# Expert products in three single passes of high and low parts, one expert after another

## What is computed

```python
order = jnp.argsort(flat_e)
tok = order // TOP_K
sizes = jnp.bincount(flat_e, length=N_EXPERTS).astype(jnp.int32)
xs = h[tok]
a = lax.ragged_dot(xs, w_gate, sizes)
u = lax.ragged_dot(xs, w_up, sizes)
y = lax.ragged_dot(jax.nn.silu(a) * u, w_down, sizes)
y = y * w.reshape(-1)[order][:, None].astype(y.dtype)
return jax.ops.segment_sum(y, tok, num_segments=n)
```

## Time and profile before

| | |
|---|---|
| median of 3 runs | 6089.7 us (6088.2 to 6094.5) |
| the profiled execution | 6090.85 us |
| its span, first to last instruction | 6089.3 us |
| jobs | 74 (36 in layer 0, 38 in layer 1), from 1,184 records of L2059 at 16 a job |
| TensorE busy | 5199.9 us, 85% of the span |
| DMA | 1111.26 MB, mean 182 GB/s |

### The profile page before, as it was taken

One profiled execution on the slowest core, in us unless ns is written; L12 is line 12 of the kernel. 1 busy time (PEld: TensorE's weight loads), 2 busy tenths in 40 slices (PEclk: granted clock), 3 DMA queues, 4 the chain that ended last, 5 costly groups with the idle time before them and its releaser, 6 DMA issues. The chain is left out here.

```text
span 6089.3 us, 76302 instructions
## 1 busy us (share of the span) xinstructions
PE 5199.9 (85%) x27165; PEld 3869.3 (64%) x27165; DVE 2233.9 (37%) x4438; ACT 1677.5 (28%) x2876; POOL 821.7 (13%) x1023
## 2 busy tenths in 40 slices
PE   9588899779789885999991888979879886999995
PEld 1388889669668763444441888978778665444442
DVE  0455155566443432111115552547553333111113
ACT  0244254446322320000001342536542221000000
POOL 0244200440000001000001440006200001000001
PEclk9799999899899997999995999989889998999998
DMA  8432451324332464899976432233343343999997
GB/s 320 175 92 88 145 172 47 95 72 111 135 147 98 167 202 165 326 335 334 334 281 229 144 95 78 68 81 78 90 134 114 143 148 110 343 334 335 334 334 265
DMA packets 610733, 1111.26 MB, mean 182 GB/s; under 512 B 108400, under 2 KB 291984, under 8 KB 610032
## 3 DMA queue, kind: packets, MB, share of 16 engines
q1 hardware_dynamic: 565104, 956.50, 47.0%
q0 software_dynamic: 29504, 94.50, 4.0%
q10 hardware_dynamic: 15936, 57.78, 2.3%
HBM read 908.23 MB, written 200.45 MB: 182 GB/s over the span
## 5 line engine op out<-in xcount | busy, mean ns | idle before, releaser
L642 PE MATMUL project_proj_acc<-project_w_split,project_hT 128*128 128x256 f32 x5472 | 720.0, 291 | 41.0 <-DVE project_w_split L527 41.0
L642 PEld LDWEIGHTS project_proj_acc<-project_w_split,project_hT 128*128 128x128 f32 x5472 | 689.5, 198 | 42.1 <-DVE project_w_split L527 41.8
L1452 PE MATMUL merge_acc<-merge_hT,merge_w_split 128*128 128x512 f32 (+1 forms) x2880 | 633.4, 376 | 20.0 <-issue 16.8
L1452 PEld LDWEIGHTS merge_acc<-merge_hT,merge_w_split 128*128 128x128 f32 x2880 | 507.9, 190 | 128.9 <-issue 22.0
L2059 PE MATMUL experts_gate_acc<-experts_w_gate,experts_rowsT 128*128 128x512 f32 x1184 | 526.0, 597 | 6.9 <-DMA experts_w_up<-in_w_exp_up_dram 6.9
L2046 PE MATMUL experts_result_acc<-experts_w_down,experts_hiddenT 128*128 128x512 f32 x1184 | 520.5, 592 | 2.4 <-DVE experts_hiddenT L2018 2.4
L2064 PE MATMUL experts_up_acc<-experts_w_up,experts_rowsT 128*128 128x512 f32 x1184 | 520.2, 592 | 0.0
L2064 PEld LDWEIGHTS experts_up_acc<-experts_w_up,experts_rowsT 128*128 128x128 f32 x1184 | 225.0, 190 | 283.2 <-issue 283.2
L2010 DVE TENSOR_TENSOR experts_hidden<-experts_silu_gate,experts_up_acc 128x512 f32<-128x512 f32 x74 | 50.9, 688 | 964.5 <-PE experts_up_acc L2064 515.4
L2059 PEld LDWEIGHTS experts_gate_acc<-experts_w_gate,experts_rowsT 128*128 128x128 f32 x1184 | 221.2, 192 | 259.1 <-issue 257.4
L2046 PEld LDWEIGHTS experts_result_acc<-experts_w_down,experts_hiddenT 128*128 128x128 f32 x1184 | 219.3, 190 | 251.6 <-issue 248.7
(11 more groups left out here) (207 smaller groups left out, 7401.2 us busy)
## 6 DMA issues: line engine op xcount, KB each, us to landing
experts_w_gate<-in_w_exp_gate_dram SPq DMA_DIRECT2D x74, 2048.0 KB, 13.8
experts_w_up<-in_w_exp_up_dram SPq DMA_DIRECT2D x74, 2048.0 KB, 18.8
experts_w_down<-in_w_exp_down_dram SPq DMA_DIRECT2D x74, 2048.0 KB, 9.8
merge_w_raw<-in_w_merge_dram SPq DMA_DIRECT2D x120, 768.0 KB, 6.6
modulation_w_ada<-in_w_ada_dram SPq DMA_DIRECT2D x24, 2048.0 KB, 7.8
qk<-project_staged SPq DMA_DIRECT2D x168, 256.0 KB, 2.3
ye<-experts_result ACTq DMA_DIRECT2D x74, 512.0 KB, 8.2
ye<-attend_a_zeros POOLq DMA_DIRECT2D x52, 512.0 KB, 27.3
```

The source lines that it names most:

```text
L642: m = pe.matmul(acc[s % 4][:, 0:HALF], hT[:, a, k, t * P:(t + 1) * P], w_split[hf][:, c, k, :], start=(i == 0 and k == 0), stop=(i == 2 an ...
L1452: m = pe.matmul(acc[:, bank, 0:w], w_split[b][:, a, k0 + k, :], act_T[:, x, kk, 0:w], start=(i == 0 and k == 0), stop=(i == 2 and k == n - 1))
```

## The change

The three products of a job become float32r products of high and low parts. The raw weights have one buffer each, in two halves (gate and up by their rows 0 to 511 and 512 to 1023, down by 0 to 255 and 256 to 511), 1 MB a half; the split weights have one buffer each. SP loads six halves a job, each when the last split that reads its buffer is done. ACT makes all high parts, DVE the low parts of five halves, POOL that of down's second half. PE runs 24 matmuls of 512 columns for each of gate, up and down. The rows and the hidden tile are split as well, and ACT copies the whole result. `deal_rows` loads the six halves of expert 0, and its list is another: jobs 0 to 31 are the first 128 rows of experts 0 to 31, and rows beyond 128 are in jobs behind them. The diff, cut to its core:

```diff
-        with ExitStack() as inner:
-            run_experts(nc, io, scr, l, nq, st, inner, ident, jobs, more_pairs)
+        with ExitStack() as weights:
+            raw = [st.sb(f"raw_{n}", [P, 2, 2048], F32, weights) for n in ("gate", "up", "down")]
+            raw_in = [[st.dma(f"raw_{n}{half}_loaded") for half in range(2)] for n in ("gate", "up", "down")]
+            with ExitStack() as inner:
+                deal_rows(nc, io, scr, l, nq, st, inner, logits, row_of, weight, jobs, more_pairs, raw, raw_in)
+            with ExitStack() as inner:
+                run_experts(nc, io, scr, l, nq, st, inner, ident, jobs, more_pairs, raw, raw_in)
         with ExitStack() as inner:
             combine(nc, io, scr, l, nq, st, inner, row_of, weight, out)
...
+            for n in range(3):
+                for half in range(2):
+                    sp.dma_start(raw[n][:, half, :], expert_half(io, l, slice(0, 1), n, half)
+                                 ).then_inc(raw_in[n][half].sem, 16)
...
             step(dve.tensor_reduce(tiles[:, :], more[:, :, :], AX.X, ALU.add))
             step(dve.tensor_tensor_scan(tiles_sum[:, :], one_row[:, :], tiles[:, :], 0.0, ALU.mult, ALU.add))
             step(dve.tensor_tensor(base[:, :], tiles_sum[:, :], tiles[:, :], ALU.subtract))
-            step(dve.tensor_scalar(base[:, :], base[:, :], float(P), None, ALU.mult))
-            step(dve.tensor_tensor(place[:, :, :], acc[:, 0:nq, :],
+            step(dve.tensor_tensor(base[:, :], base[:, :], small[:, C_JOB:C_JOB + NE], ALU.subtract))
+            step(dve.tensor_scalar(base[:, :], base[:, :], float(NE - 1), float(P), ALU.add, ALU.mult))
+            step(dve.tensor_scalar(place[:, :, :], acc[:, 0:nq, :], float(P), None, ALU.is_ge))
+            step(dve.tensor_tensor(place[:, :, :], place[:, :, :],
+                                   base[:, :].unsqueeze(1).to_broadcast([P, nq, NE]), ALU.mult))
+            step(dve.tensor_tensor(place[:, :, :], acc[:, 0:nq, :], place[:, :, :], ALU.add))
+            step(dve.tensor_scalar(base[:, :], small[:, C_JOB:C_JOB + NE], float(P), None, ALU.mult))
+            step(dve.tensor_tensor(place[:, :, :], place[:, :, :],
                                    base[:, :].unsqueeze(1).to_broadcast([P, nq, NE]), ALU.add))
...
+            step(dve.tensor_reduce(pairs_f[:, 0:1], ended[:, 0:(J - NE) // 2, 0], AX.X, ALU.add))
+            step(dve.tensor_copy(more_pairs[:, :], pairs_f[:, 0:1]))
...
+def expert_half(io, l, e, n, half):
+
+    w = io[("w_exp_gate", "w_exp_up", "w_exp_down")[n]]
+    rows = w.shape[2] // 2
+    return w[l, e, half * rows:(half + 1) * rows, :].rearrange("o (k p) n -> p (o k) n", p=P)
...
-    lo, hi = nq, MAX_JOBS // 2
-    w_gate = [sb(f"w_gate{b}", [P, KD, EH]) for b in range(2)]
-    w_up = [sb(f"w_up{b}", [P, KD, EH]) for b in range(2)]
-    w_down = [sb(f"w_down{b}", [P, HK, D]) for b in range(2)]
+    GATE, UP, DOWN = range(3)
+    PASSES = ((0, 0), (1, 0), (0, 1))
+    lo, hi = NE // 2, MAX_JOBS // 2
+    w = [sb(f"w_{n}", [P, 2, 2, 2048], F32R) for n in ("gate", "up", "down")]
...
-    xT = sb("rowsT", [P, KD, P])
+    xT = sb("rowsT", [P, 2, KD, P], F32R)
-    hT = [sb(f"hiddenT{b}", [P, HK, P]) for b in range(2)]
+    hT = sb("hiddenT", [P, 2, HK, P], F32R)
...
+    def wait_split(eng, n, half, g):
+
+        if n == DOWN and half == 1:
+            eng.wait_ge(w_lo_pool.sem, w_lo_pool.done(g))
+        elif n == DOWN:
+            eng.wait_ge(w_lo[n].sem, w_lo[n].done(g))
+        else:
+            eng.wait_ge(w_lo[n].sem, w_lo[n].done(g * 2 + half))
...
             def body(i, last):
                 for b in range(2):
                     g = i * 2 + b
+                    if isinstance(g, int) and g == 0:
+                        continue
                     e = sp.value_load(jobs[0:1, ds(g, 1)], min_val=0, max_val=NE - 1)
-                    if later(g, 2):
-                        sp.wait_ge(um.sem, um.done(g - 2))
-                    for w, name in ((w_gate, "w_exp_gate"), (w_up, "w_exp_up")):
-                        sp.dma_start(w[b][:, :, :], io[name][l, ds(e, 1), :, :].rearrange(
-                            "o (k p) n -> p (o k) n", p=P)).then_inc(gu_in[b].sem, 16)
-                    if later(g, 2):
-                        sp.wait_ge(dm.sem, dm.done(g - 2))
-                    sp.dma_start(w_down[b][:, :, :], io["w_exp_down"][l, ds(e, 1), :, :].rearrange(
-                        "o (k p) n -> p (o k) n", p=P)).then_inc(d_in[b].sem, 16)
-            pairs(sp, n, body)
+                    for n in range(3):
+                        for half in range(2):
+                            wait_split(sp, n, half, g - 1)
+                            sp.dma_start(raw[n][:, half, :], expert_half(io, l, ds(e, 1), n, half)
+                                         ).then_inc(raw_in[n][half].sem, 16)
+            pairs(sp, n_pairs, body)
...
+            def gather(g, b, i):
+                if later(i, 1):
...
             def body(i, last):
                 for b in range(2):
                     g = i * 2 + b
-                    if later(i, 1):
...
+                    if not last:
+                        gather(g + 2, b, i + 1)
+                    pool.wait_ge(w_hi[DOWN].sem, w_hi[DOWN].done(g * 2 + 1))
                     take_waits(pool, taken)
-                    pool.indirect_dma_start(
...
+                    pool.tensor_tensor(w[DOWN][:, 1, 1, :], raw[DOWN][:, 1, :], w[DOWN][:, 0, 1, :].bitcast(F32),
+                                       ALU.subtract).then_inc(w_lo_pool.sem, 1)
+            gather(0, 0, 0)
+            gather(1, 1, 0)
+            pairs(pool, n_pairs, body)
...
+            def split(n, g):
+                if later(g, 1):
+                    act.wait_ge(products[n].sem, products[n].done(g - 1))
+                for half in range(2):
+                    act.wait_ge(raw_in[n][half].sem, raw_in[n][half].done(g))
+                    act.copy(w[n][:, 0, half, :], raw[n][:, half, :]).then_inc(w_hi[n].sem, 1)
+
+            def rows_hi(g):
                 act.wait_ge(xt.sem, xt.done(g))
-                act.copy(xT[:, 0:KD // 2, :], acc_x[:, 0:D // 2].rearrange("p (k n) -> p k n", n=P)).then_inc(xa.sem, 1)
+                if later(g, 1):
+                    act.wait_ge(um.sem, um.done(g - 1))
+                act.copy(xT[:, 0, :, :], acc_x[:, :].rearrange("p (k n) -> p k n", n=P)).then_inc(xh.sem, 1)
...
-                act.copy(y[b][:, 0:D // 2], acc_y[:, 0:D // 2]).then_inc(ya.sem, 1)
-                act.wait_ge(ya.sem, ya.done(g))
+                act.copy(y[b][:, :], acc_y[:, :]).then_inc(yd.sem, 1)
                 act.wait_ge(yd.sem, yd.done(g))
                 act.dma_start(scr["ye"][ds(g * P, P), :], y[b][:, :]).then_inc(y_out[b].sem, 16)
                     if not (last and b):
-                        copy_rows(g + 1)
+                        split(GATE, g + 1)
+                        rows_hi(g + 1)
+                        split(UP, g + 1)
                     if not isinstance(g, int) or g > 0:
                         result(g - 1, 1 - b, i if b else i - 1)
-            copy_rows(0)
-            pairs(act, n, body)
-            result(n * 2 - 1, 1, n - 1)
+                    act.wait_ge(ht.sem, ht.done(g))
+                    act.copy(hT[:, 0, :, :], acc_h[:, :].rearrange("p (k n) -> p k n", n=P)).then_inc(hh.sem, 1)
+                    split(DOWN, g)
+            split(GATE, 0)
+            split(UP, 0)
+            rows_hi(0)
+            pairs(act, n_pairs, body)
+            result(n_pairs * 2 - 1, 1, n_pairs - 1)
...
+            def split(n, g):
+                for half in range(1 if n == DOWN else 2):
+                    dve.wait_ge(w_hi[n].sem, w_hi[n].done(g * 2 + half))
+                    dve.tensor_tensor(w[n][:, 1, half, :], raw[n][:, half, :], w[n][:, 0, half, :].bitcast(F32),
+                                      ALU.subtract).then_inc(w_lo[n].sem, 1)
+
+            def rows_lo(g):
+                dve.wait_ge(xh.sem, xh.done(g))
+                dve.tensor_tensor(xT[:, 1, :, :], acc_x[:, :].rearrange("p (k n) -> p k n", n=P),
+                                  xT[:, 0, :, :].bitcast(F32), ALU.subtract).then_inc(xl.sem, 1)
             def body(i, last):
                 for b in range(2):
                     g = i * 2 + b
+                    if not (last and b):
+                    if not (last and b):
...
+                        rows_lo(g + 1)
+                        split(UP, g + 1)
+                    dve.wait_ge(hh.sem, hh.done(g))
+                    dve.tensor_tensor(hT[:, 1, :, :], acc_h[:, :].rearrange("p (k n) -> p k n", n=P),
+                                      hT[:, 0, :, :].bitcast(F32), ALU.subtract).then_inc(hl.sem, 1)
+                    split(DOWN, g)
+            split(GATE, 0)
+            split(UP, 0)
+            rows_lo(0)
+            pairs(dve, n_pairs, body)
...
+            def into_hidden(n, acc, g):
+                for half in range(2):
```

(57 more changed lines are left out.)

91 lines of the change are left out of this document (38 added, 53 removed).

## The result

The changed kernel takes 6745.7 us (median of 4 runs, 6742.1 to 6747.8), the kernel before 6089.0 beside it (4 runs): 1.108 times as long, 95% interval 1.106 to 1.110. The forecast was 6650 with a range of 6525 to 6800: the sign and the mechanism held, and the increase came out at 657 us in place of 559, 97 us larger (in spans, 6745.9 - 6089.3). The rest of the text is about the order of SP's program, without which there is no loss, and about those 97 us.

What follows compares the result with a forecast made beforehand. SP's in-order wait for POOL's low half puts transfer 17.3, ACT 8.1 and POOL 4.6 in series, 30.0 us a job; 74 jobs take 2220 against 1664.7. So 6090.85 + 555 + 4 = 6650 us, range 6525 to 6800.

Steps and rivals of the forecast that it cites:

- The wait that decides: SP's in-order loads: next job's gate and up stand behind down's second half, waiting for POOL's low half; 30.0 us a job.
- the down half ahead of the five: Sign on SP's queue: one down half issued about 6 us before the five issues that follow POOL's subtraction.
- The burst, 17.3: From POOL's end to up's second half landing: hand-over 0.1, first-byte delay 2.3, five halves 13.6, gather 1.3; 17.3 us.
- the ring: Once-per-job circle through SP's waits, with transfer, ACT and POOL in series; forecast 30.0 us a job.
- POOL, 4.6: POOL's low part of down's second half with hand-over, 4.6 us a job; the subtraction itself taken as 4.5.
- DVE beside POOL: POOL slowed by DVE working beside it: 5.1 us, or 44 us in all; left out of the sum, within the range.
- ACT, 8.1: ACT's up split 2.0, result copy and store issue 1.7, hidden's high part 0.6, two down halves 3.8; 8.1 us.
- The bounds: Limits per job for the serial circle of transfer, ACT and POOL: 28.3 to 32.0 us, 126 less to 148 more.
- rival 3: Period of 33 to 35 us from slow 1 MB loads or DVE holding POOL; 6946 us, chance 11%.
- The ends: Experts stage's ends: first POOL low half 9 us above a period, last one 15 after its predecessor; cancel to a us.
- TensorE, 12 us of slack: TensorE's 18.1 us of work ends at 35, next gate due at 47; 12 us of slack hides it, cold start included.
- The list, +4: Added job-list steps ahead of the scatter: 2.0 us a layer, 4 us for both.

## Why the prediction was right, and which terms were off

- *The wait that decides* held in every link: five halves in one go behind POOL's subtraction, ACT idle for gate, POOL idle for ACT. Moving SP's waits alone turned 6746 into 5844. One sign was misplaced by its own rows: the down half ahead of the five is issued 4.4 us before POOL's end (2806.10 and 2810.53), not 6, since DVE and POOL start 1.9 apart on 2.3 and 4.5 us of work.
- *The burst, 17.3*, measured 18.8 in the mean and 19.1 in the ring shown, and is the term that was mis-sized. Its size 13.6 + 1.3 assumed the full rate after one delay of 2.3; the slices show the slow climb instead, and all of the 1.5 is there by gate's first half. From there it ran as foreseen: gate's two splits are 4.01 apart, one half of 2.72 and the 1.3 of the gather, and those at 2824.28 and 2829.64 are 5.36 apart, 2.68 a half against 2.72. The gather isn't issued right at POOL's end, as the prediction has it, but 6.2 later (2816.75), when its token numbers have landed; it still falls into the burst. That the read of the job's number is hidden beside the transfers held but for 0.3 us of a ring.
- *POOL, 4.6*, measured 5.0. The straight line gave 4.53; the median is in the row below (min, median and max ns). The Trainium skill (GPSIMD Engine Reference, "Performance versus the Vector engine") has 4497 ns for a float32 tensor_tensor of 2048 columns; this trace has 4797 on float32r output, and the measurement decides.

```profile
L1992 POOL TENSOR_TENSOR experts_w_down<-experts_raw_down,experts_w_down x74: 4747/4797/5687, 2429.3 to 6672.2; 128x2048 fp32r<-128x2048 f32 x74
```

- *DVE beside POOL* was left out since DVE's half ends near POOL's start. In the changed kernel that is so (2835.42 + 2.29 against 2837.38). Where the two did overlap, in the kernel with half the bytes, POOL took 1.0 longer for 1.3 us of overlap (5.77 is the median of its 74 there), and DVE's own 2.28 did not change. DMA traffic is not the reason: at 397 GB/s, in the kernel with the new order, POOL's subtraction took 4.79 (from 2809.05). The Trainium skill (SBUF — State Buffer, "Who interferes with whom") says that a DVE instruction with two SBUF inputs contends with a GpSimd one that reads SBUF, that the shared ports are an exclusive lock, and that the order of issue decides who blocks. If the second to start waited out the whole overlap, an estimate from that page and this trace, POOL would take 4.80 + 1.30 = 6.10; the trace agrees in which of the two pays and shows less of it, 5.78.
- *ACT, 8.1*, measured 7.6, since consecutive operations on it overlap by about 0.1.
- Sum: +1.8, -0.5 and +0.4 make the 31.7 of the ring shown, +1.5, -0.5 and +0.4 the mean of 31.3; the errors of ACT and POOL nearly cancel, so the burst is the miss. Over both stages the rings inside are 31.25 in the mean, and 74 x 1.25 = 93 of the 97 us missed. The bounds (28.3 to 32.0) held it. The lower one was added up wrong: its terms, 1.3, 0.4 and 0.2, give 28.1 and 6509; nothing hangs on it here. The mark that I had set for rival 3, up's second half landing later than 19 us after the burst began, was nearly reached (the split behind that landing starts at 18.8 in the mean); its 33 us were not.
- *The ends*, foreseen to cancel, make up the other 4 us or so: the last gap between two POOL subtractions is 17.7 us in layer 0 and 17.2 in layer 1, where 15 was foreseen, and the first low half of layer 0 ends 74.5 us behind the first scatter, where 30.9 to the start as before and 39 made 70; shorter last steps give a part of it back.
- *TensorE, 12 us of slack*, and 10 with a cold start: its idle in the ring shown is 10.45 us, and the gate group behind it takes 7.69 in place of 5.8, so the cold start costs 2. The granted clock is 0.50 (the level of 1.2 GHz) at the start of that group and nearly full in its last part, as two stretches show (busy us of TensorE, then granted clock, DMA share and GB/s). It is hidden, as the kernel with one product shows.

```profile
2830.40:2832.00 1.60, 1.60 (x4) 0.50 0.00 0
2834.00:2838.00 4.00, 4.00 (x18) 0.95 0.18 75
```

- *The list, +4*: the first scatter comes at 2360.50 where the one of before came at 2354.72; counted from DVE's copy of the rank product it is 1.95 later, foreseen 2.0 (2352.85 and 2349.02; the rest of the shift lies ahead of that, in stages that the change doesn't touch). In the time of the whole it can't be seen.

## What to carry to other kernels

An in-order queue that issues loads must not hold a wait for the last step of a job ahead of loads whose buffers came free long before; order its issues by when their buffers come free. Such a ring shows itself when no engine and no queue is full and the long waits name one another round a circle; add its links in series, not the busy times. And test the order first: here it was worth 901 us, 13% of the changed kernel, with the same loads, splits and products.

## What was not expected of the hardware

- With the queue never empty, 1 MB loads, 0.5 MB gathers and stores together moved 397 GB/s for hundreds of us, above the 385 read from a short stretch.
- A burst into an empty queue took some 5 us from its first traffic to that rate, with slices as low as 49 GB/s in between. Its second half-load was there 1.5 us later than one delay plus bytes over rate would have it, and 1.7 later when each load was half as large.
- POOL's subtraction grew from 4.80 to 5.78 us with 1.3 us of a DVE subtraction over it, and DVE's own length stayed.
